# A hybrid encoder layer: DeltaNet decays by repeated row reads, two products in f16 parts, the gate projection spread through the chunks, gates ahead of the normalising

## The chip, the cores and the metric

The kernel runs on one core of one Trainium2 chip. The metric is the device time of one execution in microseconds, the median of the runs shown; lower is better.

## The reference, cut to what matters

One layer of an encoder trunk (1024 tokens, width 1024): four mixers read one projection of the normalised input, their outputs are gated and merged, then come cross attention to a memory of 256 tokens and a mixture of 32 experts. The change touches the fourth mixer, a bidirectional gated DeltaNet (4 heads of width 64), and the merge.

```python
def gdn_scan(q, k, v, beta, log_a):
    gam = jnp.cumsum(gc, axis=-1)
    diff = gam[..., :, None] - gam[..., None, :]
    decay = jnp.exp(jnp.where(incl, diff, -jnp.inf))
    kk = jnp.einsum('bhntd,bhnsd->bhnts', kc, kc)
    a_mat = jnp.where(strict, bc[..., None] * kk * decay, 0.0) + jnp.eye(c)
    rhs = jnp.concatenate([vc * bc[..., None], kc * (bc * jnp.exp(gam))[..., None]], axis=-1)
    sol = lax.linalg.triangular_solve(a_mat, rhs, left_side=True, lower=True, unit_diagonal=True)
    qk = jnp.einsum('bhntd,bhnsd->bhnts', qc, kc) * decay
    q_dec = qc * jnp.exp(gam)[..., None]
    def step(state, inp):
        v_new = u_i - jnp.einsum('bhtd,bhde->bhte', kc_i, state)
        o = jnp.einsum('bhtd,bhde->bhte', qd_i, state) + jnp.einsum('bhts,bhse->bhte', qk_i, v_new)
        state = cd_i[..., None, None] * state + jnp.einsum('bhsd,bhse->bhde', kd_i, v_new)
...
def gdn_mixer(...):
    o = rmsnorm(o_f + o_b, norm_g) * jax.nn.silu(z)
...
def gated_merge(h, branches, merge_w, merge_b, branch_up):
    for i, y in enumerate(branches):
        term = jax.nn.sigmoid(h @ merge_w[i] + merge_b[i]) * (y @ branch_up[i])
        out = term if out is None else out + term
```

## The kernel before

The whole layer is one program. `plan_schedule` writes out one list of steps by hand, and each engine walks through this list in order and does its share of each step; between engines there are only semaphore waits. Each engine, and each engine's own DMA queue, is thus in order.

**Dense work.** Every large product is a panel of weights, 256 columns wide, named by what it makes: `nz` is the DeltaNet's output gate projection z, `merge20` to `merge23` the merge of the third mixer, `early1` and `early2` the middle merge gates of the fourth, `merge30` its first two tiles (gates and `up` products), `late3` the `up` products of the middle tiles, `merge33` the last two tiles. Weights are split into two f16 parts, and each product is three f16 matmuls. For this SyncE loads two rows of weight tiles (a chunk, "conv") into one of four landing slots (L1260), ScalarE makes the high part (L1358), VectorE (or GpSimd in some panels) the low part (L1944). The chunks of a panel are spread through the parts of the panel before it; the first stands ahead of its first part. A part is 6 matmuls of 128x512 or 12 of 128x256. Every group of four parts fills one of two PSUM banks, used in turn, and the next user of a bank waits until it has been emptied ("evac"): a gate by ScalarE with a tanh (L1379), an `up` product by VectorE. `dense(..., between=...)` puts the parts into a list: each `None` in `between` is a place for one part, every other entry is a step of the mixers.

**DeltaNet.** 8 chunks of 128 tokens, two directions `d` of 4 heads. `gdn_gam` makes the running sums of the log decays and their exponentials. `gdn_a` i makes for chunk i the decayed blocks: part 0 forms the differences of the running sums by one f32 product with a triangular matrix (L979; GpSimd writes its right side at L2793) and the exponential (L1707), GpSimd masks it (L2799), part 1 makes the key and query products (L989) which VectorE scales (L2367, L2375), part 2 a transpose (L996) and copies of the diagonal blocks (L1715). The blocks go to memory (L1747) and are read back later. `gdn_inv` are steps of VectorE (L2385, L2388) that invert the 32x32 diagonal blocks of half the chunks; 10 such steps for the first half stand in and behind the last `gdn_a`, 10 for the second half in the first three `gdn_c`. `gdn_c` i has seven parts:

- 0: the decay of the queries by a product (GpSimd L2820, TensorE L1014, exponential L1725), GpSimd spreads the inverted blocks into block matrices (L2807), first level of the inverse (L1023), negated by VectorE (L2406)
- 1 to 3: the other products of the inverse (L1033, L1040, L1023), copied by VectorE and ScalarE
- 4: its product with the keys (L1047)
- 5: its product with the values, f32 (L1053), less that with the state (L1061); VectorE scales the new values
- 6: the state's addition (L1067), the output from the state (L1072) and from the new values, f32 (L1075); VectorE updates the state (L2429) and adds the output (L2432; for the first four chunks ScalarE stores it)

After the recurrence `fin` squares, sums and normalises the output (VectorE's gain product is L2227), `fin_gate` multiplies by silu of the `nz` result (L2235), `fin_tr` transposes it (L889) into Y, which the `up` products of the fourth mixer read. `early_in` makes SyncE wait for the gain product and then read back eight stored gates (L1281), which the `late3` evacuations use.

## Time and profile before

| | us |
|---|---|
| median of 3 runs (2063.43 to 2067.67) | 2064.29 |
| the profiled execution, its own time | 2065.67 |
| its span, first to last instruction | 2063.9 |
| TensorE busy | 1909.5 |
| VectorE busy | 1388.5 |
| ScalarE busy | 1083.7 |
| GpSimd busy | 324.1 |

The mean granted TensorE clock was 0.971 of full speed. Busy is the time that at least one instruction of an engine covers; as matmuls are pipelined, the time that a group of them costs is read from the chain, which gives their issue times. An f32 matmul has two records. The stretches: `gdn_a` some 673 to 754 us, `gdn_c` 792.3 to 954.9 us, `nz` to 975.8 us, `merge30` from there.

### The profile page before, as it was taken

Reading aid. Unit: us, or ns where it says so; the run is one execution under the profiler, and the core shown is the slowest. Engines: PE = TensorE matmul, PEld = TensorE weight load, DVE = VectorE, ACT = ScalarE, POOL = GpSimd, SP = SyncE. Lnnn points to the kernel's source line nnn. Section 1 sums busy time; section 2 is a strip of 40 time slices with the busy share of each in tenths; the row PEclk is TensorE's granted clock in tenths of the full one; section 3 lists DMA queues with packets and bytes.
Section 4 is the critical chain, followed back from the end, with each engine's and each line's share of the span. In section 5 each row is a group of like instructions: output and inputs, shape, how many; then the busy total and the mean of one; then the engine's idle time right before and its main releaser. Section 6 shows DMA issues by size and latency. Waiting matters only on the chain.

```text
span 2063.9 us, 33015 instructions
## 1 busy us (share of the span) xinstructions
PE 1909.5 (93%) x13076; PEld 1138.2 (55%) x13076; DVE 1388.5 (67%) x1831; ACT 1083.7 (53%) x1582; POOL 324.1 (16%) x285
## 2 busy tenths in 40 slices
PE   6999999999999999999999999895899999999991
PEld 3464565655544545767488855685355444444440
DVE  4555533799865687634643845437799999999986
ACT  4563223666656432223333534334588888888862
POOL 6000100344300523421000000000001111111102
PEclk9999999999999999999999999997899999999995
DMA  5411111212011352332321500403799999999976
GB/s 185 161 51 42 32 42 53 66 47 57 24 39 47 118 179 83 113 108 99 138 67 48 168 32 21 167 31 152 268 423 422 422 422 421 422 422 422 422 290 261
DMA packets 140522, 360.45 MB, mean 175 GB/s; under 512 B 38224, under 2 KB 91632, under 8 KB 113776
## 3 DMA queue, kind: packets, MB, share of 16 engines
q1 hardware_dynamic: 96608, 279.57, 35.7%
q10 hardware_dynamic: 34944, 46.14, 6.4%
q0 software_dynamic: 8848, 33.03, 4.1%
q8 instruction: 87, 1.43, 0.3%
q14 instruction: 35, 0.29, 0.0%
HBM read 307.85 MB, written 46.66 MB: 172 GB/s over the span
## 4 chain that ended last, share of the span: by engine, by line
PE 79%; DVE 9%; ACT 5%; issue 4%; DMA 1%; SPq 1%; DVEq 0%; ACTq 0%; POOL 0%; POOLq 0%
PE psum L787 40%; PE psum L1194 24%; ACT arena L1636 2%; PE psum L1183 1%; PE psum L1118 1%; PE psum L1093 1%; DVE arena L2288 1%; PE psum L917 1%; PE psum L1212 1%; PE psum L804 1%; PE psum L1053 1%; PE psum L989 1%; DMA arena<-in_w_in_dram 1%; PE psum L979 1%; PE psum L928 1%
## 5 line engine op out<-in xcount | busy, mean ns | idle before, releaser
L787 PE MATMUL psum<-arena 128*128 128x512 f16 (+2 forms) x6000 | 1016.6, 327 | 7.7 <-issue 2.8
L787 PEld LDWEIGHTS psum<-arena 128*128 128x128 f16 x6000 | 569.6, 98 | 391.5 <-issue 23.5
L1194 PE MATMUL psum<-arena 128*128 128x512 f16 x2304 | 513.5, 382 | 15.6 <-issue 12.5
L744 DVE SCALAR_TENSOR_TENSOR arena<-arena 128x2048 f16<-128x2048 f32 x192 | 437.6, 2286 | 57.9 <-ACT arena L738 57.6
L738 ACT ACTIVATE arena<-arena 128x2048 f16<-128x2048 f32 x192 | 365.5, 1908 | 69.6 <-DMA arena<-in_w_dram 42.9
L1194 PEld LDWEIGHTS psum<-arena 128*128 128x128 f16 x2304 | 224.7, 98 | 282.4 <-issue 24.7
L1944 DVE SCALAR_TENSOR_TENSOR arena<-arena 128x512 f16<-128x512 f32 (+1 forms) x185 | 124.9, 695 | 123.0 <-ACT arena L1358 122.6
L2847 POOL DMA_INDIRECT arena<-xhat,arena x32 | 67.5, 2109 | 842.1 <-PE psum L1183 446.0
L1358 ACT ACTIVATE arena<-arena 128x512 f16<-128x512 f32 (+1 forms) x212 | 127.0, 616 | 35.8 <-PE psum L787 11.4
L1379 ACT ACTIVATE arena<-psum,arena 128x512 f32<-128x512 f32 x64 | 43.8, 684 | 149.2 <-PE psum L787 149.1
L1443 ACT ACTIVATE arena<-psum 128x512 f32<-128x512 f32 (+3 forms) x51 | 29.9, 586 | 119.8 <-PE psum L787 119.8
L1407 ACT ACTIVATE arena<-arena 128x256 f32<-128x256 f32 x64 | 26.6, 416 | 108.9 <-DVE arena L1980 107.9
L2735 POOL TENSOR_SCALAR arena<-arena 128x512 f32<-128x512 f32 x27 | 57.5, 2129 | 138.8 <-ACT arena L1358 138.8
L2273 DVE CUSTOM_DVE_ANT_0 arena<-psum,arena 128x1024 f32<-128x1024 f32 x64 | 75.6, 1219 | 2.1 <-PE psum L904 2.0
L1968 DVE SCALAR_TENSOR_TENSOR arena<-arena,psum 128x512 f32<-128x512 f32 x64 | 43.8, 684 | 49.0 <-PE psum L787 34.8
L1636 ACT ACTIVATE arena<-arena 128x1024 f32<-128x1024 f32 x64 | 72.9, 1147 | 7.1 <-DVE arena L2273 7.0
L1998 DVE SCALAR_TENSOR_TENSOR arena<-psum,arena 128x512 f16<-128x512 f32 x36 | 24.8, 690 | 61.5 <-ACT arena L1443 31.0
L1980 DVE SCALAR_TENSOR_TENSOR arena<-psum,arena 128x512 f32<-128x512 f32 x32 | 22.1, 690 | 64.3 <-PE psum L787 64.3
L1645 ACT ACTIVATE arena<-psum 128x512 f16<-128x512 f32 x64 | 34.7, 595 | 55.1 <-PE psum L917 34.3
L2807 POOL TENSOR_TENSOR arena<-arena 128x512 f32<-128x512 f32 x32 | 34.8, 1106 | 128.0 <-DMA arena<-gdn_inv 82.6
L1859 ACT ACTIVATE arena<-psum 128x512 f32<-128x512 f32 x64 | 38.1, 597 | 14.2 <-PE psum L1194 13.9
L1183 PE MATMUL psum<-arena 128*128 128x128 f32 x256 | 34.4, 278 | 10.3 <-DMA arena<-xhat,arena 10.3
(390 smaller groups left out, 2089.6 us busy)
## 6 DMA issues: line engine op xcount, KB each, us to landing
arena<-in_w_dram SPq DMA_DIRECT2D x192, 1024.0 KB, 11.9
arena<-in_merge_w_dram SPq DMA_DIRECT2D x64, 256.0 KB, 3.0
yrows<-arena ACTq DMA_DIRECT2D x32, 512.0 KB, 7.9
arena<-in_w_in_dram SPq DMA_DIRECT2D x48, 256.0 KB, 2.8
gdn_lq<-arena ACTq DMA_DIRECT2D x8, 1024.0 KB, 4.0
arena<-gdn_lq ACTq DMA_DIRECT2D x8, 1024.0 KB, 5.1
arena<-in_xattn_wkv_dram SPq DMA_DIRECT2D x32, 256.0 KB, 2.8
yrows<-arena POOLq DMA_DIRECT2D x1, 7680.0 KB, 24.3
```

What stands on the lines that cost most here:

```text
L738: nc.scalar.activation(half_of(pieces(e, m)[0], half), half_of(XLAND[m], half), ACT.Copy, scale=WS).then_inc(w_hi[m], 1)
L744: nc.vector.scalar_tensor_tensor(half_of(lo, half), half_of(XLAND[m], half), WS, half_of(hi, half), ALU.mult, ALU.subtract).then_inc(w_lo[ ...
L787: mm = nc.tensor.matmul(bank[prt[0]:prt[1], c0:c1], lhs[a](k), rhs[b](k), start=(k == 0 and a + b == 0), stop=(k == nk - 1 and a == 1))
L1183: tr = nc.tensor.transpose(PS[:, k // 4, (k % 4) * P:(k % 4) * P + P], xs[:, k, :], ident)
L1194: mm = nc.tensor.matmul(PS[:, bank, :], left[a][:, k, :], right[b][:, k, columns], start=k + a + b == 0, stop=(k == n - 1 and a == 1))
L1358: S.activation(W[i % 2][0][:, 2 * j:2 * j + 2, 0:wide], LAND[c % NLAND][:, :, 0:wide], ACT.Copy, scale=WS).then_inc(*act_hi.mark(c))
L1379: S.activation(SG[gate_no[n] % 2], bank, ACT.Tanh, scale=0.5 / WS, bias=half_b[:, 8 * kind[1] + kind[2]:8 * kind[1] + kind[2] + 1]).then_i ...
L1636: S.activation(DS[u % 2][:, m, :], DS[u % 2][:, m, :], ACT.Exp, scale=-1.0, bias=d_mx[u % 2][:, m:m + 1], accum_out=d_l[u % 2][:, m:m + 1])\
L1944: V.scalar_tensor_tensor(W[i % 2][1][:, 2 * j:2 * j + 2, 0:wide], LAND[c % NLAND][:, :, 0:wide], WS, W[i % 2][0][:, 2 * j:2 * j + 2, 0:wid ...
L2273: V.tensor_tensor_reduce(out=DS[u % 2][:, m, :], in0=PS[:, 2 + 2 * m:4 + 2 * m, :].rearrange("p a b -> p (a b)"), in1=DWH[:, 896 - P * qt: ...
L2735: G.tensor_scalar(landed_c, landed_c, WS, None, ALU.mult).then_inc(*counter("pool_w_scaled").mark(chunk))
L2847: G.indirect_dma_start(XR[e % 2], None, XH_D, bass.IndirectOffsetOnAxis(IDX[:, e:e + 1], 0)).then_inc(rows_in[e % 2], 16)
```

## The change

1. **Decays.** A new step `gdn_rows` transposes the running sums (64 rows of 128), and ScalarE writes them and their exponentials to memory. `gdn_a` part 0 no longer has a product: DMAs of ScalarE's queue read the four rows of a chunk and direction into all 128 partitions, ScalarE makes Relu(column - row) per head and the exponential of its negative. `gdn_first` issues the first reads, the others are issued two chunks ahead. In `gdn_c` part 0 four DMAs per chunk bring the exponentials of the rows for the queries; VectorE waits for them in part 4. GpSimd's L2793 and L2820, and TensorE's L979 and L1014, are gone.
2. **f16 parts.** The products of the inverse with the values (part 5) and of the decayed scores with the new values (part 6) become three f16 matmuls each. Their operands are split: ScalarE makes the high, VectorE the low parts (`zh`, `zl`, `qh`, `ql`, `vh`, `vl` per chunk and direction, the values once). The output's products move behind the state products of both directions, and the state's update waits only for the latter (`qs`).
3. **Order.** `nz` is no longer a stretch of its own: `gdn_a` 0 to 5 and `gdn_c` get 16 more places. The panel merge30 has its four gates first and then its four `up` products; they begin at once after the recurrence, with `fin_tr` after 11 of their parts. The four gates go where the stored gates would go, not into the two slots. `early_in` waits for the gating product instead of the gain product. `merged_pair` 0 moves from merge30 to merge33.

```diff
-PAIRS_AT = {(3, 1, 0, 2): [(0, 2)], (3, 6, 0, 1): [(1, 2)], ...
+PAIRS_AT = {(3, 6, 0, 0): [(0, 2)], (3, 6, 0, 1): [(1, 2)], ...
...
-            if (i, q) != (3, 0):
+            if (i, q) == (3, 0):
+                pairs = pairs[::2] + pairs[1::2]
+            else:
...
-        gdn += [("gdn_a", i, 1)] + {...}.get(i, []) + [None] + [("gdn_a", i + 1, 0), None] * (i + 1 < TT) + mid
+        gdn += [("gdn_a", i, 1)] + {...}.get(i, []) + [None] * (1 + (i < 6)) + [("gdn_a", i + 1, 0), None] * (i + 1 < TT) + mid
...
-            gdn += [("gdn_c", i, part)] + [None] * (1 <= part < 6)
+            gdn += [("gdn_c", i, part)] + [None] * (part < 6 + (i < 2))
...
-    dense("nq", "nk", "nv", *merge(2), *[f"early{q}" for q in (1, 2)], between=gdn)
-    dense("nz", between=[("fin", "gdn")])
-    order += [("fin_gate", "gdn"), ("early_in",)]
+    dense("nq", "nk", "nv", *merge(2), *[f"early{q}" for q in (1, 2)], "nz", between=gdn)
...
-    dense(*merge(3), between=[None] * 4 + [("fin_tr", "gdn"), ("mem_again",)] + [None] * 16 + [("mem_stats",)] + again)
+    dense(*merge(3), between=[("fin", "gdn"), ("fin_gate", "gdn"), ("early_in",)] + [None] * 11 + [("fin_tr", "gdn"), ("mem_again",)]
+          + [None] * 12 + [("mem_stats",)] + again)
...
-                            nc.tensor.matmul(B0[:, :, :], st_f if d else st_b, NX[d], start=True, stop=True)\
-                                .then_inc(*q.mark("seg", i, d))
...
-                                nc.tensor.matmul(PS[:, 3 + 3 * d, h * 64:h * 64 + 64], NZ_[d][:, SLOT_OF[h], :],
-                                                 NVT[:, c, h * 64:h * 64 + 64], start=h == 0, stop=False)
+                                for x, y in ((0, 0), (0, 1), (1, 0)):
+                                    nc.tensor.matmul(PS[:, 3 + 3 * d, h * 64:h * 64 + 64], NZP[d][x][:, SLOT_OF[h], :],
+                                                     NVP[y][:, c, h * 64:h * 64 + 64], start=h + x + y == 0, stop=False)
...
+                            mm.then_inc(*q.mark("qs", i, d))
+                    if part == 6:
+                        for d in range(2):
+                            pe.wait_ge(*v.at("ql", i, d))
+                            pe.wait_ge(*v.at("vl", i, d))
                             for h in range(NH):
+                                for x, y in ((0, 0), (0, 1), (1, 0)):
+                                    mm = nc.tensor.matmul(PS[:, 2 + 3 * d, h * 64:h * 64 + 64], NQP[s][d][x][:, SLOT_OF[h], :],
...
-                    sp.wait_ge(*counter("vec_fin").at("g", "gdn"))
+                    sp.wait_ge(*counter("vec_fin").at("done", "gdn"))
...
+                            act.wait_ge(gam_in[i % 2], 32 * (i // 2) + 32)
+                            for h in range(NH):
+                                S.activation(NGR[i][d][:, h, :], NGR[i][d][:, h, :], ACT.Relu, scale=-1.0, bias=GAS[:, d, c, h:h + 1])\
...
+                            S.activation(NY[d], NGR[i][d], ACT.Exp, scale=-1.0).then_inc(*a.mark("dt", i, d))
...
+                                S.activation(NZP[d][0], NZ_[d], ACT.Copy, scale=WS).then_inc(*a.mark("zh", i, d))
...
+                            S.activation(NNP[d][0], NVN[d], ACT.Copy).then_inc(*a.mark("vh", i, d))
...
+                            S.activation(NQP[i % 2][d][0], NQT[i % 2][d], ACT.Copy, scale=WS).then_inc(*a.mark("qh", i, d))
...
+                            V.scalar_tensor_tensor(NZP[d][1], NZ_[d], WS, NZP[d][0], ALU.mult, ALU.subtract).then_inc(*v.mark("zl", i, d))
...
+                            V.scalar_tensor_tensor(NQP[i % 2][d][1], NQT[i % 2][d], WS, NQP[i % 2][d][0], ALU.mult, ALU.subtract).then_inc(*v.mark("ql", i, d))
...
+                            V.tensor_tensor(NNP[d][1], NVN[d], NNP[d][0], ALU.subtract).then_inc(*v.mark("vl", i, d))
...
+                S.activation(early_gate(kind), bank, ACT.Tanh, scale=0.5 / WS, ...
```

## Rows read from the trace of the kernel before

**Rows 1.** The page: busy us, share and instructions of each engine.
```profile
PE 1909.5 (93%) x13076; PEld 1138.2 (55%) x13076; DVE 1388.5 (67%) x1831; ACT 1083.7 (53%) x1582; POOL 324.1 (16%) x285
```

**Rows 2.** Busy times by stretch: length, then busy us (instructions) of each engine.
```profile
673.00:752.00 79.00, 76.69 (x515) 42.85 (x514) 55.19 (x86) 35.95 (x88) 39.81 (x32) 1.00 0.38 131
...
790.00:955.00 165.00, 155.09 (x1791) 114.53 (x1790) 93.03 (x246) 39.08 (x91) 58.59 (x79) 0.99 0.29 86
```

**Rows 3.** The chain that ended last, 950 to 1400 us: start, us, what.
```profile
954.86 20.97 PE psum L787 x192
...
979.71 2.30 DVE arena L2235
```

**Rows 4.** Timeline of all engines, 948 to 992 us: start, duration, what.
```profile
955.50 0.42 DVE L2432 TENSOR_TENSOR arena<-psum,arena 128x256 f32<-128x256 f32 x1
...
966.91 3.67 SPq L1281 DMA_DIRECT2D arena<-early_gates  x8
...
970.63 0.80 SPq L1260 DMA_DIRECT2D arena<-in_branch_up_dram  x1
...
979.58 0.61 ACT L1358 ACTIVATE arena<-arena 128x512 f16<-128x512 f32 x1
...
981.04 0.69 ACT L1379 ACTIVATE arena<-psum,arena 128x512 f32<-128x512 f32 x1 [0.84 <-PE psum L787]
...
982.05 1.97 PE L889 MATMUL psum<-arena 128*128 128x128 f32 x16 [1.05 <-DVE arena L2235]
```

**Rows 5.** TensorE's waits, 790 to 992 us.
```profile
PE psum L1033 <- DVE arena L2406: 4.4, 8, 1.5
```

**Rows 6.** The chain that ended last, 560 to 955 us: start, us, what.
```profile
573.33 0.70 PE psum L928 x24
...
681.94 1.72 PE psum L979 x4
...
805.19 0.84 PE psum L1053 x8
...
812.68 0.50 PE psum L1014 x4
```

**Rows 7.** TensorE's instructions by line, 790 to 955 us.
```profile
L1075 PE MATMUL psum<-arena 128*128 128x64 f32 x128 | 16.1, 268 | 0.0
```

**Rows 8.** Busy times, last two chunks of `gdn_a`.
```profile
731.00:754.00 23.00, 19.89 (x137) 11.17 (x136) 20.49 (x39) 8.89 (x23) 7.28 (x6) 1.00 0.26 104
```

**Rows 9.** ScalarE's instructions by line, 673 to 955 us.
```profile
L1715 ACT ACTIVATE arena<-arena 32x128 f32<-32x128 f32 x32 | 9.8, 307 | 0.8
```

**Rows 10.** Timeline of GpSimd and VectorE, 731 to 800 us.
```profile
733.24 2.50 POOL L2793 TENSOR_TENSOR arena<-arena 128x512 f32<-128x512 f32 x2
...
733.77 1.02 DVE L2385 TENSOR_TENSOR arena<-arena 128x30 f32<-128x30 f32 x1
...
758.19 0.69 DVE L1944 SCALAR_TENSOR_TENSOR arena<-arena 128x512 f16<-128x512 f32 x1
...
798.56 0.20 DVE L2385 TENSOR_TENSOR arena<-arena 128x30 f32<-128x30 f32 x1
```

**Rows 11.** Busy times of the first four chunks of `gdn_c`.
```profile
792.30:812.50 20.20, 18.70 (x223) 13.97 (x223) 15.61 (x41) 4.54 (x11) 9.77 (x13) 1.00 0.06 19
812.50:833.00 20.50, 18.96 (x224) 14.10 (x224) 17.98 (x45) 5.01 (x12) 6.91 (x9) 1.00 0.28 78
833.00:854.00 21.00, 19.03 (x224) 14.17 (x224) 16.69 (x45) 5.54 (x13) 7.75 (x11) 1.00 0.35 102
854.00:874.00 20.00, 19.53 (x228) 14.69 (x227) 8.52 (x24) 6.14 (x14) 8.74 (x14) 1.00 0.49 159
```

**Rows 12.** DMAs that read branch_up weights, 940 to 1000 us.
```profile
DMA to landing us min/median/max: 3.0/6.3/7.5
```

**Rows 13.** Busy times, 2 us in `gdn_c` after a wait; the column PEclk.
```profile
895.00:897.00 2.00, 1.61 (x64) 1.38 (x66) 1.32 (x6) 0.38 (x1) 0.72 (x2) 1.00 0.03 8
897.00:899.00 2.00, 2.00 (x24) 0.86 (x15) 1.30 (x5) 0.00 (x0) 0.00 (x0) 0.54 0.00 0
```

174 lines of the change are left out of this document (105 added, 69 removed).

## The prediction

> **What bounds it now.** I read the page first: TensorE is busy for 93% of the span [rows 1]. The edits lie between 673 us and 992 us, so the busy times by stretch come next: in the stretch that forms the decays and the triangular blocks, TensorE works 76.7 us of 79; in the stretch of `gdn_c`, 155.1 of 165; VectorE is at 93.0 of 165 there, as a mean [rows 2]. By the chain, the recurrence ends at 954.86 us, the `nz` projection then takes 20.97 us of unbroken TensorE work, and of the normalising only a 1.05 us wait for the gating product is left open in front of `fin_tr` [rows 3, 4]. So TensorE bounds this part: a matmul taken out shortens it, one moved does not, and idle time is worth filling only where there is some. By the list of waits, the largest in `gdn_c` is 4.4 us behind VectorE's negated blocks, among 9.9 us of idle in all (165 less 155.1) [rows 2, 5].
>
> **What is taken out of TensorE.** The prices are issue times of the chain [rows 6]. The segment sum in `gdn_a` costs 1.72 us per chunk (two of 128x512 f32, four records), 13.8 us over 8 chunks. The decay product in `gdn_c` costs 0.50 us per direction, 16 times: 8.0 us. The two f32 products against 64-column values cost 0.84 us per direction for 8 records; 128 records of the second [rows 7], as many of the first (8 chunks, 2 directions, 4 heads, 2 records), make 16 groups each, 32 x 0.84 = 26.9 us. In their place stand 12 f16 matmuls of the same 128x64 shape per group; the chain has 24 of them in 0.70 us, so 0.35 us, 32 times: 11.2 us. The new transpose is one matmul. Net: 13.8 + 8.0 + 26.9 - 11.2 = 37.5 us less TensorE work.
>
> The segment sum's two weight loads lie inside the 1.72 us. The Trainium skill (TensorE: Matmul & The Clock Gate, Weight-path perf modes) says that fast weight load is off for FP32, which is why the f16 form can gain by more than its three products lose; the trace agrees (0.84 against 0.35 us), and by the page alone the sum would be the same.
>
> **What is moved.** The 16 parts of `nz` (1.31 us each, 20.97 / 16) go into 6 new places in `gdn_a` and 10 in `gdn_c`. That is the same TensorE work; it gains only where it falls on idle time. `gdn_a` then changes per chunk by 1.31 - 1.72 = -0.4 us, for six chunks -2.5 us; in the last two VectorE is the busy one (20.5 of 23 us, [rows 8]), so the 3.4 us of their segment sums I take as nothing, with -3 us as the other end. `gdn_c` 0 begins at 792.3 - 2.5 = 789.8 us.
>
> The decays now come by repeated reads. In `gdn_a` ScalarE gains eight Relu of 128x128 and two DMA issues per chunk. The nearest row for a small activation is 0.31 us [rows 9], so some 3 us a chunk, 25 us on an engine that has 36 of 79 us busy [rows 2]; the rows are read two chunks (18 us) ahead. I cost this at nothing; if that cover failed, each chunk would wait some 2 us, 16 us in all. GpSimd loses `tla` and `lab`, which is slack it had; its cost to VectorE is weighed below.
>
> **`gdn_c`, the disputed term.** Before, 8 chunks took 162.6 us (792.3 to 954.86). Without 8.0 + 26.9 - 11.2 = 23.7 us and with 10 places of 1.31 us it is 152.0 us if the waits stay. They will not stay. VectorE gets six new operations per chunk: four low halves of 128x512 at 0.69 us [rows 10] and two of 128x256 at about 0.4 [rows 4], or 3.5 us. The first three chunks, which also hold the inverses of the second half, have VectorE at 15.6, 18.0 and 16.7 us of 20.2 to 21 [rows 11]: 19.1, 21.5 and 20.2 after. TensorE would need only 19.9, 20.2 and 19.4 us. VectorE is late there, and with the handoffs that an engine at its limit cannot hide (today 1.5 to 2 us per chunk) I take 20.9, 22.6 and 21.5 = 65.0 us. In the last five (VectorE 8.5 + 3.5 us in the row of the first of them, of some 18.4) TensorE leads: 100.9 before (854.0 to 954.86), less 5 x 2.96 = 14.8, plus 6.5 = 92.6, and for the two new handoffs (values to f16 on ScalarE, the rest on VectorE, both ahead of the state update in VectorE's order) 0.5 us a chunk: 95.1. Together 160 us. From both sides: 142 us if even the old waits vanish (152.0 - 9.9); 172 us if VectorE's added 28 us all fall on the path and the new places absorb only 8 of them.
>
> Here a rule speaks against the change. The rows show an operation of 30 elements on VectorE taking 1.02 us where the same form takes 0.20 us, and the long one stands while GpSimd multiplies [rows 10]. The Trainium skill (SBUF — State Buffer, Who interferes with whom) says that a VectorE operation with two SBUF inputs and a GpSimd operation that reads SBUF exclude each other for the whole instruction. All six new low halves have two SBUF inputs, and those of the values come while GpSimd spreads the blocks of the next chunk. By row one such meeting costs 0.8 us; two a chunk would be 13 us over the stage, the upper half of my bound, while the loss of `tla` and `lab` gives some back.
>
> **The end of the recurrence, where a new wait appears.** After it, the order is `fin`, `fin_gate`, `early_in`, and then the gates of merge30 with 11 places before `fin_tr`. Let E be the end of the last product, 789.8 + 160 = 949.8 us. VectorE's part as now: the last sum 1.06 us after E; from there to the early-gate reads, which now stand behind the gain product, 11.0 us (966.91 less 955.92) [rows 4]. In the new order they stand behind the gating product too, 2.3 us more [rows 3]: E + 14.4. Eight issues take 3.67 us: E + 18.0. Only then can SyncE issue the next panel's weights, late3 chunk 0, which is behind them in its order. The same pair today: issued at 970.63, and the landings of this tensor take 3.0 to 7.5 us, the middle one 6.3, behind the 2 MB of gates [rows 4, 12]. So the weights land at E + 24.3.
>
> On ScalarE the conversion of that chunk stands ahead of the tanh of the first gate (it is the first step of merge30's first part). So the first bank is empty at E + 24.3 + 0.6 + 0.7 = E + 25.6 [rows 4]. TensorE fills two banks in 8 parts, 8 x 1.31 = 10.5 us, and must then wait: 15.1 us. Queued behind it: two gates, `fin_tr`, everything. Before, this order did no harm, because `nz` covered the time in which VectorE normalised and loads went out. On top: after a far shorter gap (1.6 of 2 us busy) the granted clock stood at 0.54 for the next 2 us [rows 13], so for most of it the lower of the levels 1.2 and 2.4 GHz; some 4 us at it would cost 2 us, which I add. `fin_tr` itself is then no longer waited for (-1.05).
>
> **Sum.** Before, the gates of merge30 begin at 954.86 + 20.97 = 975.83, with 1.05 us to wait: 976.9. After: 949.8 + 15.1 + 2 = 966.9. Gain 10.0 us against the profiled execution of 2065.67 us (span 2063.9): 2055.7. That execution lies 1.4 us over the median of 2064.29, so 2054.3 us; I say 2055. Everything after merge30 waits for it, so the gain arrives whole. The eighth pair (`merged_pair` 0) in merge33 costs ScalarE and VectorE about a microsecond each beside gates of 5 us: nothing.
>
> **Rivals.**
> (a) The hold behind `early_in` does not come or is short (the weights land as soon as the first landings do, or SyncE is released earlier). For it: TensorE had no such hold in the trace. Against: one queue each on SyncE and ScalarE, both in order. Then 2055 - 17 = 2038 us.
> (b) Slower: VectorE becomes the bound of all of `gdn_c`, by the low halves and their exclusion by GpSimd. The change breaks even when 976.9 = 789.8 + C + 17.1, that is at C = 170.0 us, 21.3 a chunk against 20.3 now. For it: the first chunks have VectorE nearly full. Against: the later ones have it below half. At C = 175, 2070 us. By the skill's exclusion rule alone C is 160 + 13 = 173, 2067 us.
> (c) The fill is worth nothing and the products gain nothing, because waits take their place one for one, the hold included: near 2064 us. What speaks for it is that each freed microsecond in `gdn_c` lies next to a handoff; against, that 13.8 us of segment sums have no new handoff on TensorE.
>
> **How the numbers follow.** Forecast (hold and C of 150 to 166) 0.64, its own range 2045 to 2061; (a) 0.14; (b) 0.13; (c) 0.09. About 0.2% (4 us) is what a measurement of this kernel can tell from no change. Faster takes the forecast nearly whole and (a), 0.77; the same 0.10; slower 0.13. The range reaches to (a), and to C = 172: 2037 to 2067.
>
> **What would show it.** After the recurrence: a gap on TensorE of about 15 us, eight parts behind its end, with ScalarE's conversion waiting for a branch_up DMA; no gap refutes it. `gdn_c`: about 160 us, its first three chunks longer than the rest, VectorE over 90% in them, f16 groups of 12 in about 0.35 us. `gdn_a`: no f32 128x512 product, chunks of 9.0 us. I am wrong if ScalarE is late with the Relus, if the row reads land late, or if the hold is not there.

## The result and the profile after

The changed kernel takes 2082.94 us (median of 5 runs, 2078.02 to 2087.12) against 2064.29 us (median of 5 runs beside it, 2063.22 to 2071.28): a ratio of 1.0084, 95% interval 1.0059 to 1.0110. It is slower by 0.8%, where 2055 us was forecast with a range of 2037 to 2067. The profiled execution is the longest of the five, 2087.12 us (span 2085.4); the one of before took 2065.67. One execution of experiment e9 took 8630.36 us, against 2054.86 to 2063.89 us of the other eight, and is left out of its ratio.

The page first: busy us and share of each engine, as in [rows 1].

```profile
PE 1888.3 (91%) x13109; PEld 1117.6 (54%) x13109; DVE 1424.9 (68%) x1883; ACT 1121.1 (54%) x1680; POOL 302.0 (14%) x253
```

TensorE does 21.2 us less and the kernel takes 21.5 us more, so some 43 us of idle time are new. The busy times by stretch say where. Columns as in [rows 2]; the stretches are `gdn_a`, the first two intervals of `gdn_c`, its third, the rest of it, and the time after the recurrence.

```profile
678.50:801.10 122.60, 108.02 (x679) 58.28 (x678) 84.20 (x153) 63.37 (x168) 27.10 (x23) 0.96 0.56 175
801.10:849.00 47.90, 37.37 (x450) 24.56 (x450) 42.62 (x97) 15.44 (x33) 12.62 (x14) 0.92 0.25 69
849.00:876.00 27.00, 20.73 (x245) 14.10 (x245) 20.62 (x51) 7.87 (x17) 7.40 (x8) 0.88 0.30 90
876.00:980.70 104.70, 94.20 (x1306) 72.07 (x1306) 67.00 (x148) 37.41 (x80) 31.20 (x36) 0.92 0.31 94
980.70:1004.00 23.30, 10.35 (x48) 4.51 (x46) 10.50 (x8) 8.16 (x9) 0.00 (x0) 0.80 0.41 134
```

The columns are the stretch, its length, the busy us (and instructions) of TensorE, its weight loads, VectorE, ScalarE and GpSimd, then TensorE's granted clock and two columns on DMA. TensorE is idle for 14.6 of the 122.6 us of `gdn_a`, for 27.3 of the 179.6 us of `gdn_c` and for 13 us right after it. VectorE is busy for 63.2 of the first 74.9 us of `gdn_c` (84%) and for 67.0 of the other 104.7 us (64%). The list of TensorE's waits, 670 to 1015 us (what waits, for whom: us in total, times, longest), names the holders:

```profile
PE psum L1071 <- DVE arena L2474: 15.4, 3, 6.3
PE psum L797 <- ACT arena L1382: 13.0, 1, 13.0
PE psum L996 <- ACT arena L1753: 8.7, 5, 2.3
PE psum L1026 <- DVE arena L2496: 8.1, 3, 3.4
PE psum L1003 <- DVE arena L2427: 5.9, 1, 5.9
PE psum L1049 <- ACT arena L1775: 2.2, 4, 0.9
PE psum L1085 <- DVE arena L2493: 0.6, 1, 0.6
```

Before, the largest was 4.4 us in eight pieces [rows 5]. L1071 (the state's addition, L1067 before) waits for VectorE's new values (L2474), three times: in the chunks that hold the inverses. L1026 (first level of the next chunk's inverse) waits for VectorE's sum of the output (L2496), since it writes the bank that the sum reads. L996 (the key products of `gdn_a`) waits for ScalarE's diagonal copies (L1753), and L1003 (its transposes), once, in the last chunk, for VectorE's scaled products (L2427); these two make up the 14.6 us of `gdn_a`. L797 is dense work, the gates of merge30; its one wait of 13.0 us is the hold.

These measures repeat below, all from the traces: `gdn_a`, from its first key product to the first product of the inverse in `gdn_c`; `gdn_c`, from there to E, the end of its last output product; inside it the seven intervals between the starts of the eight chunks' products with the state (L1076); and "to the router", from the first key product to a product of the expert routing behind all edits (L1161, L1151 before), 751.2 us before and 769.9 us after. They scatter: the changed kernel, e1 and e2 have the same code in `gdn_c` and show 179.4, 177.2 and 175.4 us, so that a difference of 2 to 4 us in `gdn_c` between two traces says little by itself.

| us | before | after | forecast |
|---|---|---|---|
| `gdn_a` | 114.4 | 122.6 | 111.3 |
| `gdn_c` | 161.7 | 179.4 | 160 |
| E to the gates (`nz` included before) | 22.0 | 0 | 0 |
| hold and slow clock behind it | 0 | 13.0 + 2.1 | 15.1 + 2 |

The forecast's 111.3 us is 789.8 less 678.5 us; its 160 us counts from 792.3 us in the kernel before, where the stage is 162.6 us long.

**The hold**, in the chain that ended last (start, us, what):

```profile
981.57 1.92 ACT arena L1613
...
983.51 2.30 DVE arena L2265
...
986.44 2.30 DVE arena L2267
...
988.77 2.30 DVE arena L2274
...
991.17 2.30 DVE arena L2282
993.48 0.35 SPq L1291
...
997.20 5.56 DMA arena<-in_branch_up_dram
...
1003.32 0.68 ACT arena L1382
```

The last output group ends at 980.53 us. VectorE's gating product ends at 993.47, SyncE then issues eight reads of early gates (L1291) and only then the next panel's weights, which land at 1002.76; ScalarE converts them ahead of the first gate's tanh (L1382). TensorE fills its two banks and stands from 991.05 to 1004.04.

**A late chunk of `gdn_c`**, the timeline of all engines (start, duration, what):

```profile
953.90 4.91 POOL L2862 TENSOR_TENSOR arena<-arena 128x512 f32<-128x512 f32 x4 [12.99 <-PE psum L1065]
...
954.58 0.76 DVE L2474 SCALAR_TENSOR_TENSOR arena<-psum,arena 128x256 f32<-128x256 f32 x2
...
955.49 2.42 DVE L2493 TENSOR_TENSOR arena<-arena 128x256 f16<-128x256 f32 x2
...
957.62 0.94 PE L1085 MATMUL psum<-arena 128*128 128x64 f16 x24
957.83 0.41 DVE L2479 TENSOR_TENSOR arena<-psum,arena 128x256 f32<-128x256 f32 x1
...
958.27 0.94 DVE L2484 SCALAR_TENSOR_TENSOR arena<-arena 128x128 f32<-128x128 f32 x2
...
960.60 0.74 DVE L2496 SCALAR_TENSOR_TENSOR arena<-psum,arena 128x256 f32<-128x256 f32 x2
...
961.11 0.97 PE L1026 MATMUL psum<-arena 32*32 32x32 f32 x32 [2.55 <-DVE arena L2496]
```

From the new values (954.58) everything up to the next chunk's first product stands in VectorE's order: low halves (L2493), masks and state (L2479, L2484), sums (L2496). TensorE's output products (L1085) are done by 958.6 us, and it then stands for 2.55 us. The pair of low halves takes 2.42 us while GpSimd spreads blocks (L2862).

### The profile page after: what moved, and what is told of

Same layout as the page of the kernel before. It is cut to its first block, busy times and chain, and to the rows that moved or that the text cites. A ratio compares the mean times of both kernels' runs of the same rounds, so it can differ in the third digit from the quotient of the medians.

```text
span 2085.4 us, 33231 instructions
## 1 busy us (share of the span) xinstructions
PE 1888.3 (91%) x13109; PEld 1117.6 (54%) x13109; DVE 1424.9 (68%) x1883; ACT 1121.1 (54%) x1680; POOL 302.0 (14%) x253
## 4 chain that ended last, share of the span: by engine, by line
PE 75%; DVE 11%; ACT 6%; issue 5%; DMA 2%; SPq 1%; DVEq 1%; ACTq 0%; POOLq 0%
PE psum L797 38%; PE psum L1204 24%; ACT arena L1650 2%; PE psum L1193 1%; PE psum L1128 1%; PE psum L1103 1%; DVE arena L2335 1%; PE psum L927 1%; PE psum L996 1%; PE psum L1222 1%; PE psum L814 1%; DVE arena L2437 1%; DVE arena L2440 1%; ACT arena L1735 1%; DMA arena<-in_w_in_dram 1%
## 5 line engine op out<-in xcount | busy, mean ns | idle before, releaser
L797 PE MATMUL psum<-arena 128*128 128x512 f16 (+2 forms) x6000 | 1022.8, 328 | 20.9 <-ACT arena L1382 13.0
L797 PEld LDWEIGHTS psum<-arena 128*128 128x128 f16 x6000 | 570.9, 99 | 406.3 <-issue 22.6
L1204 PE MATMUL psum<-arena 128*128 128x512 f16 x2304 | 513.7, 382 | 15.1 <-issue 12.0
L1368 ACT ACTIVATE arena<-arena 128x512 f16<-128x512 f32 (+1 forms) x212 | 127.3, 616 | 64.1 <-issue 15.4
L1394 ACT ACTIVATE arena<-psum,arena 128x512 f32<-128x512 f32 x60 | 41.1, 684 | 133.3 <-PE psum L797 133.1
L2027 DVE SCALAR_TENSOR_TENSOR arena<-psum,arena 128x512 f32<-128x512 f32 x32 | 22.1, 690 | 64.6 <-PE psum L797 64.6
L2862 POOL TENSOR_TENSOR arena<-arena 128x512 f32<-128x512 f32 x32 | 38.1, 1219 | 128.1 <-DMA arena<-gdn_inv 67.1
## 6 DMA issues: line engine op xcount, KB each, us to landing
yrows<-arena POOLq DMA_DIRECT2D x1, 7680.0 KB, 24.3
```

Of the source, the lines that this page charges most:

```text
L797: mm = nc.tensor.matmul(bank[prt[0]:prt[1], c0:c1], lhs[a](k), rhs[b](k), start=(k == 0 and a + b == 0), stop=(k == nk - 1 and a == 1))
L1204: mm = nc.tensor.matmul(PS[:, bank, :], left[a][:, k, :], right[b][:, k, columns], start=k + a + b == 0, stop=(k == n - 1 and a == 1))
L1368: S.activation(W[i % 2][0][:, 2 * j:2 * j + 2, 0:wide], LAND[c % NLAND][:, :, 0:wide], ACT.Copy, scale=WS).then_inc(*act_hi.mark(c))
```

## The experiments

Ratios are to the kernel before, measured beside each run on the same chip, with 95% intervals. The quotient of the two medians can lie up to 0.23% beside the ratio; where that matters it is given too. Two kernels are compared by their ratios; many of these pairs come from different chips, and the changed kernel's 1.0084 was measured apart from the experiments. "Base" is the kernel that an edit is made to.

### Each suspect of the change by itself (base: the changed kernel)

**e1**: the early gates' reads stand nine parts later.

```diff
-    dense(*merge(3), between=[("fin", "gdn"), ("fin_gate", "gdn"), ("early_in",)] + [None] * 11 + ...
+    dense(*merge(3), between=[("fin", "gdn"), ("fin_gate", "gdn")] + [None] * 9 + [("early_in",)] + [None] * 2 + ...
```

> The changed kernel with one step moved: SyncE's wait for the gating product (early_in) stands behind nine parts of merge30 instead of ahead of them, so that both weight chunks of the next panel are issued before it. Theory (the 13.0 us gap behind the recurrence is this order alone): the wait of TensorE for the tanh of the first gate goes from 13.0 us to under 1 us, and the time falls from 2083 to about 2070 us. Rival (the gap would be there anyway, because VectorE is still normalising): a wait of about the same length stands in front of the transposes, and the time falls by less than 4 us.

Measured: 0.9998 [0.9982, 1.0014]. The wait for L1382 is gone from the list, the others stay within 1 us. By ratio the hold is worth 0.86%, some 18 us, for a wait of 13.0 us and 2.1 us of slow clock behind it; from E to the router the traces are 18.3 us apart. The 3 us beyond the priced 15.1 were not traced.

**e2**: ScalarE's Relus and exponentials of the next chunk behind the diagonal copies.

```diff
-  ... [("gdn_a", i + 1, 0), None] * (i + 1 < TT) + mid
-        gdn += [("gdn_a", i, 2), ("gdn_out", i)]
+  ... [None] * (i + 1 < TT) + mid
+        gdn += [("gdn_a", i, 2)] + [("gdn_a", i + 1, 0)] * (i + 1 < TT) + [("gdn_out", i)]
```

> The changed kernel with ScalarE's share of gdn_a part 0 (eight Relu, two exponentials, two row reads) moved behind the copies of the diagonal blocks of the chunk before; TensorE's order is the same, as part 0 has no product any more. Theory (TensorE's 8.7 us of waits for those copies come from the Relus ahead of them in ScalarE's order): gdn_a takes about 9 us less, 2074 us. Rival (ScalarE's total is the bound of gdn_a, so the wait only changes its place: the masks of GpSimd come later and VectorE's scaling waits for them): within 3 us of 2083.

Measured: 1.0084 [1.0058, 1.0109] (by the medians 1.0075), `gdn_a` 121.9 us: the 9 us are not there. Its list of waits has no L996 any more, but the wait at L1003 grew from 5.9 to 11.2 us: the decays come late instead.

```profile
PE psum L1003 <- DVE arena L2427: 11.2, 5, 6.7
```

This order took no work off ScalarE's queue, it only chose what is late.

**e3** and **e4**: one product back in f32, with all of its parts, waits and scales: the output's in e3 (first edit), the values' in e4 (second).

```diff
-                                for x, y in ((0, 0), (0, 1), (1, 0)):
-                                    mm = nc.tensor.matmul(PS[:, 2 + 3 * d, h * 64:h * 64 + 64], NQP[s][d][x][:, SLOT_OF[h], :],
+                                mm = nc.tensor.matmul(PS[:, 2 + 3 * d, h * 64:h * 64 + 64], NQT[s][d][:, SLOT_OF[h], :],
...
-                                for x, y in ((0, 0), (0, 1), (1, 0)):
-                                    nc.tensor.matmul(PS[:, 3 + 3 * d, h * 64:h * 64 + 64], NZP[d][x][:, SLOT_OF[h], :],
+                                nc.tensor.matmul(PS[:, 3 + 3 * d, h * 64:h * 64 + 64], NZ_[d][:, SLOT_OF[h], :],
```

> The changed kernel with the output's product (decayed scores with new values) back in f32: without qh, ql, vh, vl, with 6.7 us more of TensorE work (16 groups at 0.84 instead of about 0.42 us). Theory (VectorE's order and its exclusion by GpSimd's spreading bound gdn_c): gdn_c falls from 179.6 us to about 168, the pair of low halves of the new values that took 2.42 us is gone, 2071 us. Rival (TensorE bounds gdn_c): 2090 us.

> The changed kernel with the product of the inverse with the values back in f32: without zh, zl and the low half of the values, with 6.7 us more of TensorE work. Theory (what hurts is low halves on VectorE where it is full or meets GpSimd; zl stands in part 3, while TensorE has two parts to do): a small gain in the first three chunks, about as much lost in the last five, 2078 to 2084 us. Rival one (every low half costs its full time, 1.4 us a chunk, and the conversions of ScalarE too): 2072 us. Rival two (TensorE bounds): 2090 us.

Measured: e3 1.0029 [1.0016, 1.0043], `gdn_c` 167.7 us (168 forecast); e4 1.0056 [1.0035, 1.0077], `gdn_c` 174.3 us, between its theory and its first rival. TensorE as the bound is refuted in both. The output's f16 form is a loss; for the values' form the interval overlaps the changed kernel's, and it alone is less sure.

### Taken together, and the order alone

**e5**: both products in f32 (the edits of e3 and e4). **e6**: e5 with the edit of e1. **e7**: the kernel before with only the new order (nz spread, gates first, kept gates). **e8**: e7 with the edit of e1.

> The changed kernel with both 64-column products back in f32 (no f16 parts of either; the row reads, the spread of the gate projection and the new order after the recurrence stay). Theory 1 (f16 parts are a loss here, because the matmul time they save is less than the VectorE and ScalarE work and the handoffs they put ahead of TensorE's next step, and the two losses are separate): the two single reversals add up, 0.55% and 0.28% below the changed kernel, so a ratio to the kernel before of about 1.000, and gdn_c falls from 179.6 to some 162 us. Rival 2 (the losses have one common cause, a VectorE that is full in the first chunks, so that taking either product's parts away already removes it): no more than the larger single one, a ratio near 1.003. Rival 3 (the f16 form does save once VectorE is free): the ratio is above 1.003.

> As the run before it, and the reads of the early gates stand behind nine more parts of merge30, so that SyncE issues the next panel's weights first. Theory 1 (the hold is 13 us whatever the recurrence does): 13 to 17 us less than the run before it, a ratio near 0.992, some 2040 us against 2056 before, and the wait for ScalarE's tanh of the kept gate is gone. Rival (with the recurrence shorter the reads are issued earlier and the hold was shorter already): less than 8 us between the two.

> The kernel before with only the new order: the gate projection nz spread through the chunks, the gates of merge30 over the normalising, the kept gates; decays by products and both products in f32 as before. Theory 1 (spread parts fill only the idle time there is, 9.9 us in gdn_c, and the hold behind early_in costs 13 us): nz's 21 us cost the recurrence some 14 to 16 us, the hold 13: slower than before by about 6 us, ratio 1.001 to 1.005. Rival 1 (the spread parts fill nothing): 12 us slower, 1.006. Rival 2 (the hold does not come without the row reads): ratio 0.995 to 0.998.

> The run before it with the early gates' reads later. Theory 1: 13 us less, so some 7 us below the kernel before, ratio 0.996 to 0.998. Then the difference between this run and e6 is what the row reads for the decays bring alone: by the matmul time they save 21.8 us, by the 8.7 us of waits for ScalarE in gdn_a and its longer chunks about 8 us; if e6 is not below this run, the row reads bring nothing.

| | ratio | `gdn_a`, us | `gdn_c`, us | L1071 or its like, us | hold, us |
|---|---|---|---|---|---|
| e5 | 1.0003 [0.9992, 1.0014] | 123.1 | 168.1 | 4.4 | 12.5 |
| e6 | 0.9953 [0.9929, 0.9977] | 122.9 | 168.0 | 3.9 | 0 |
| e7 | 1.0071 [1.0047, 1.0095] | 120.8 | 173.2 | 5.8 | 13.6 |
| e8 | 0.9985 [0.9971, 0.9999] | 121.4 | 172.1 | 5.0 | 0.4 |

By ratio the two single reversals add up (0.55% and 0.28%, together 0.81%), as theory 1 said; in `gdn_c` they don't (168.1 us, no shorter than e3's 167.7, and 162 was forecast). Whether the values' parts cost anything without the output's is thus open. The hold is worth 0.50% from e5 to e6, 10 us where 13 to 17 were forecast, and 0.86% from e7 to e8; from E to the router the traces give 14.1 and 14.8 us. The order alone is slower by 0.7% (0.1 to 0.5% forecast), and the hold is all of it: without it e8 is no slower than before. Sixteen parts of `nz` lengthen `gdn_a` by 6.4 and `gdn_c` by 11.5 us, 17.9 of their 21: spreading them filled 3 us. e6 to e8, where neither has a hold, gives the row reads 0.3% (by the traces 2.8 us to the router), e5 to e7 0.7% (3.7 us); the intervals overlap, and neither is the 21.8 us of matmuls that they remove.

### What in the f16 form costs

**e9** (base: the changed kernel): GpSimd's spreads cut to one column for chunks 3 to 7; part of the blocks is left out.

```diff
+                            if i < 3:
                                 spread(NX[d], d, d).then_inc(*po.mark("x", i, d))
                                 spread(NZ_[d], 1 - d, d).then_inc(*po.mark("z", i, d))
+                                continue
+                            G.tensor_copy(NX[d][:, :, 0:1], XZC[s][:, 8 * d + 4 * d:8 * d + 4 * d + 4, 0:1]).then_inc(*po.mark("x", i, d))
+                            G.tensor_copy(NZ_[d][:, :, 0:1], XZC[s][:, 8 - 4 * d:12 - 4 * d, 0:1]).then_inc(*po.mark("z", i, d))
```

> The changed kernel, but for the last five chunks of gdn_c GpSimd's four spreads of the next blocks (1.23 us each) are cut to a copy of one column, so that this part of the blocks is left out of the computation. Theory 1 (GpSimd's spread and VectorE's low half of the values exclude each other, the pair takes 2.42 us in place of 0.84, and VectorE's order behind it sets when the next chunk's y may start): the pair takes 0.8 to 0.9 us in these chunks, the wait of L1026 for DVE falls by about 1.5 us a chunk, gdn_c by 6 to 8 us from 179.4, ratio about 1.005. Rival (VectorE is not what sets the end there, or the pair is long for another reason): pair and gdn_c stay, ratio 1.008.

Measured: 0.9984 [0.9969, 0.9999], `gdn_c` 161.4 us, 18.0 less and over twice the forecast. The same pair and the first state updates in its timeline, and two of its waits:

```profile
938.62 0.76 DVE L2493 TENSOR_TENSOR arena<-arena 128x256 f16<-128x256 f32 x2 [0.15 <-ACT arena L1785]
...
940.14 0.61 DVE L2484 SCALAR_TENSOR_TENSOR arena<-arena 128x128 f32<-128x128 f32 x2
```
```profile
PE psum L1071 <- DVE arena L2474: 11.5, 3, 4.5
...
PE psum L1026 <- DVE arena L2496: 3.4, 3, 1.2
```

The pair takes 0.76 us in place of 2.42 us, so GpSimd's work was what stretched it. The Trainium skill (SBUF — State Buffer, Who interferes with whom) says that an operation with two SBUF inputs and a GpSimd operation that reads SBUF lock each other out for the whole instruction. The trace agrees: beside the last spread (to 958.81 us) the changed kernel's mask, with one input in PSUM, took 0.41 us, against 0.42 here, while the pair of state updates behind it, with two SBUF inputs, took 0.94 us against 0.61 here. But the stretched pairs make up only 2 us a chunk; how 18.0 us come of them is not shown by this run.

**e10** (base: the changed kernel): f16 output product of high halves alone, the low halves left out.

```diff
-                            pe.wait_ge(*v.at("ql", i, d))
-                            pe.wait_ge(*v.at("vl", i, d))
+                            pe.wait_ge(*a.at("qh", i, d))
+                            pe.wait_ge(*a.at("vh", i, d))
...
-                            V.scalar_tensor_tensor(NQP[i % 2][d][1], NQT[i % 2][d], WS, NQP[i % 2][d][0], ALU.mult, ALU.subtract)...
-                            V.tensor_tensor(NNP[d][1], NVN[d], NNP[d][0], ALU.subtract)...
...
```

> The changed kernel with the output product still as 12 f16 matmuls a group, but all of the high halves; the four low halves of it (two of 128x512, two of 128x256 on VectorE) are left out. Theory 1 (VectorE's low halves and what is queued behind them are the loss): gdn_c falls by more than the 11.7 us that the f32 form brought, since the shorter f16 group stays: 162 to 166 us, ratio 1.001 or below. Rival (ScalarE's high halves and the longer chain of handoffs from the values to the group are the loss): gdn_c stays above 172 us, ratio above 1.005.

Measured: 1.0038 [1.0024, 1.0051], `gdn_c` 169.8 us: between the two. Leaving out the low halves gives 9.6 of the 11.7 us that the f32 form brings. This kernel still has f16 groups that are 0.49 us shorter than e3's, 7.8 us over 16 groups, and yet it is no shorter than e3. By subtraction ScalarE's high halves and the handoffs behind them cost some 10 us; no run cuts them alone.

**e11** (base: the changed kernel): VectorE's sums ahead of masks and state.

```diff
+                    for d in range(2 * (part == 6 and i >= 4)):
+                        dve.wait_ge(*q.at("o", i, d))
+                        V.scalar_tensor_tensor(NO[:, c, :], PS[:, 2 + 3 * d, 0:256], 1 / WS, NO[:, c, :], ...
```

> The changed kernel with one order changed: in the chunks in which VectorE adds the output (the last four), the two sums stand ahead of the masking and the state update in its order, not behind them. Theory 1 (the bank of the next y is free late, since the sum waits behind 2.9 us of masking and state update, which themselves wait behind the low halves): the 8.1 us of waits of L1026 for the sum fall to under 3 us, gdn_c by 3 to 5 us, ratio about 1.006. Rival (the state update is as urgent: GpSimd's products with it come late and hold the next chunk): the wait moves to the state or the key products, no gain, 1.008.

Measured: 1.0050 [1.0032, 1.0068], `gdn_c` 170.7 us, 8.7 less (3 to 5 forecast). The last three intervals fall from 21.4, 21.8 and 22.2 to 19.0, 18.8 and 19.2 us; the first two stay at 27.0 and 26.9. L1026 waits for the sum no more; 3.3 us of waits turned up at the next product of the inverse (L1035), and the state was not urgent. The hold grew from 13.0 to 15.0 us, so that 6.2 us of the 8.7 are left at the router (0.34%, 7 us, by ratio).

**e13** (base: the changed kernel): the parts formed, the f32 product used without waiting for them, its scale left out.

> The changed kernel in which all f16 parts of the output product are still formed, but the product is the f32 one of 8 records a group and waits for none of them (the scale of that product is left out, so the output is not the reference's). Theory 1 (VectorE's operations for the parts delay the mask, the state and the next chunk whether the product waits for them or not): gdn_c stays within 4 us of the changed kernel's 179.4, ratio 1.007 to 1.010. Rival (it is the product's wait for the low halves, and the parts by themselves would be hidden): gdn_c falls towards the 167.7 of the f32 form, ratio below 1.005.

Measured: 1.0076 [1.0052, 1.0101] (by the medians 1.0090), `gdn_c` 184.8 us: 5.4 us above the changed kernel, where at most 4 us were forecast, with 7.8 us of longer products in it. The rival is refuted: the work for the parts delays the chunk whether or not the product waits for it.

**e17** (base: e6): the cut of e9 where there are no output or value parts.

> The kernel of e6 (both products f32, early gates read later), GpSimd's spreads cut in the last five chunks as in e9 (part of the blocks is left out of the computation). Theory 1 (the 18 us of e9 come of the exclusion and VectorE's order, which bind only with the low halves): gdn_c within 3 us of e6's 168.0. Rival (the spreads load VectorE and the clock whatever the product's form): gdn_c falls by 6 us or more, to 162 or less.

Measured: 0.9893 [0.9872, 0.9913], `gdn_c` 159.5 us, 8.5 less than e6. The forecast of 3 us was wrong, the rival's 6 us or more came. Its last four intervals are 19.6, 19.2, 19.2 and 19.2 us against e6's 19.6, 19.4, 19.8 and 19.8: 1.4 us. Almost all the rest falls in the second and third (24.6 and 24.2 to 20.9 and 21.1), and one wait accounts for half of it:

```profile
PE psum L1069 <- DVE arena L2453: 3.9, 1, 3.9
```
```profile
PE psum L1069 <- DVE arena L2453: 0.6, 1, 0.6
```

(e6, then e17.) There VectorE has the inverses to do and meets the spread of the first cut chunk. In the last four intervals of the f16 form the same cut had given 12.2 us (84.0 less 71.8). I read this so: GpSimd's spreads cost VectorE time in both forms, and it reaches the end only where VectorE's order is what the next chunk waits for: in the inverse chunks, or everywhere once the f16 parts are in it. That fits both runs; a spread that is moved instead of cut would test it.

### Row reads, Relus, and the best form of each

**e12** (base: e6): `gdn_a`'s decays by the segment-sum product again, `gdn_c`'s by row reads.

```diff
+                        if part == 0:
+                            pe.wait_ge(*po.at("tla", i, d))
+                            nc.tensor.matmul(B0[:, :, :], st_f if d else st_b, NX[d], start=True, stop=True)...
-                                S.activation(NGR[i][d][:, h, :], NGR[i][d][:, h, :], ACT.Relu, ...
-                            S.activation(NY[d], NGR[i][d], ACT.Exp, scale=-1.0)...
+                            S.activation(NY[d], PS[:, 2 + 3 * d, :]..., ACT.Exp)...
```

> The kernel of e6 (both products f32, early gates read later) with gdn_a's decays by the segment-sum product again, as before the change; gdn_c's still come by row reads. Theory 1 (in gdn_a the row reads gain nothing, since the 13.8 us of products are replaced by waits for ScalarE's Relus): within 3 us of e6, either side, ratio 0.994 to 0.997, and TensorE is busy in all of gdn_a's first chunks of 10.7 to 10.9 us. Rival (the product's matmuls did bound gdn_a): 8 to 14 us slower than e6, ratio about 1.000.

Measured: 0.9942 [0.9924, 0.9961], `gdn_a` 123.1 us, e6 has 122.9. Taking 13.8 us of products out of `gdn_a` was worth nothing. What the row reads bring is in `gdn_c`, 166.3 us here against 172.1 in e8, with 8.0 us of products gone.

**e15** (base: e6): the Relus' work on GpSimd.

```diff
-                                S.activation(NGR[i][d][:, h, :], ..., ACT.Relu, scale=-1.0, bias=GAS[:, d, c, h:h + 1])...
+                            G.tensor_tensor(NGR[i][d], NGR[i][d], bc(GAS[:, d, c_, :]...), ALU.subtract)...
+                            G.tensor_scalar(NGR[i][d], NGR[i][d], 0.0, None, ALU.min)...
```

> The kernel of e6 (both products f32, early gates read later) with the lower bound of the differences formed on GpSimd (a subtraction and a minimum of 128x512 a direction) in place of ScalarE's eight Relus a chunk. Theory 1 (the Relus ahead of the diagonal copies in ScalarE's order are what lengthens gdn_a): the 8.7 us of waits of L996 for ScalarE go, gdn_a's chunks fall from 10.9 to 9.5 us or less, 6 to 9 us less than e6, ratio 0.991 to 0.993. Rival (GpSimd and VectorE exclude each other here, and VectorE is late in its place): PE waits for VectorE's products, gdn_a no shorter, ratio 0.995 or above.

Measured: 0.9893 [0.9864, 0.9922], `gdn_a` 118.8, `gdn_c` 165.3. The medians, 2042.96 us against 2060.34, give 0.9916. Of the kernels that compute the whole layer it has the lowest ratio, but e18's interval overlaps its own and e18's medians give the same 0.9916. By its list of waits L996 waits for ScalarE once, and VectorE is next:

```profile
PE psum L1003 <- DVE arena L2406: 6.1, 3, 5.0
...
PE psum L996 <- ACT arena L1745: 3.3, 1, 3.3
```

`gdn_a` gave 4.1 us, not the 6 to 9 forecast, and `gdn_c` 2.7; to the router it is 6.8 us shorter than e6. GpSimd is busy for 70.7 us of `gdn_a` in place of 27.3, and VectorE, with as many instructions (153), for 92.4 in place of 84.1: the rival's wait was there too (L1003), at a price smaller than the gain.

**e14** (base: the changed kernel): e1's and e11's edits, and f16 output only from chunk 3 on. **e16**: e14 without row reads in `gdn_a`. **e18**: e14 with e15's edit.

```diff
+                                if i < 3:
+                                    mm = nc.tensor.matmul(PS[:, 2 + 3 * d, h * 64:h * 64 + 64], NQT[s][d][:, SLOT_OF[h], :],
...
+                                    continue
```

> The changed kernel with three edits: early gates read later, the output sums first in VectorE's order, and the output product in f16 parts only from chunk 3 on, in f32 in the three chunks that hold the inverses. Theory 1 (in those chunks VectorE is full, and each operation added there is added to the path; in the others the low halves are hidden once the sums come first): the first two intervals between the chunks' products fall from 27.0 and 26.8 to about 22 and 24.5, as in the f32 form, the later ones stay at 19; gdn_c 163 to 166 us, ratio 0.990 to 0.994. Rival (the f16 values are what holds the first chunks): the first intervals stay above 25, gdn_c about 170, ratio 0.996.

> The kernel of e14 with gdn_a's decays by the segment-sum product, as before the change. Theory 1 (the row reads are neutral there): within 3 us of e14. Rival: 5 us or more slower, since TensorE's 13.8 us come back.

> The kernel of e14 (f16 values everywhere, f16 output from chunk 3 on, sums first, early gates read later) with the lower bound formed on GpSimd as in e15. Theory 1 (the f16 parts bring nothing even with everything else mended, since their shorter groups are paid with VectorE's and ScalarE's work): within 4 us of e15's ratio of 0.9893, either side. Rival (the f16 parts' 0.4 us a group show once nothing else is in the way): 5 to 8 us below e15, ratio about 0.986.

Measured: e14 0.9954 [0.9924, 0.9985], `gdn_c` 169.1 us, first intervals 25.4 and 24.3; e16 0.9979 [0.9959, 0.9998]; e18 0.9921 [0.9903, 0.9939], `gdn_c` 165.5 us. e14 was forecast at 163 to 166 us and 0.990 to 0.994. The second interval came as forecast, the first (22 forecast) did not; it is 24.6 in e16 and 22.2 in e18, as in e3 (22.1), so it isn't the f16 values, and its cause was not found. e16 lies 5 us above e14 by ratio, with overlapping intervals, and 0.8 us by the traces to the router: between its theory and its rival the runs don't decide. e18 was forecast within 4 us of e15 and is 5.8 us above it by ratio, again with overlapping intervals, and 0.1 us by the traces to the router (733.8 against 733.7); the rival, f16 5 to 8 us ahead, is refuted. Even with all that was found mended, f16 parts end where f32 does (169.1 against 168.0, 165.5 against 165.3). The f32 forms never had the sums first, which might have helped them too.

## Why the prediction was wrong

Three steps failed. "A matmul taken out shortens it", by which TensorE alone bounds this part; "I cost this at nothing" for ScalarE's new work in `gdn_a`, which came out 11.3 us later than forecast; and the 160 us of `gdn_c`, which took 179.4, because VectorE's order between two chunks was priced at 0.5 us of handoffs. The hold, the price of the f16 groups and the clock behind the hold were right.

**What TensorE is relieved of.** Right as a price: the chain of the changed kernel has the f16 group at 0.35 us.

```profile
952.94 0.35 PE psum L1057 x12
```

But 37.5 us less matmul work showed as 21.2 us less busy time. Up to the end of the recurrence the granted clock is 0.88 to 0.96 in the stretches above, against 1.00 and 0.99 in [rows 2]; two waits behind which dense work ran slower are shown below. The step "a matmul taken out shortens it" is the first that failed: it holds only as long as nobody else is as late as TensorE, and here ScalarE and VectorE were. e12 shows it plainly: with or without the 13.8 us of segment sums `gdn_a` takes 123 us. Rival (c) had this mechanism, and what the prediction set against it, that the segment sums had no new handoff, is what failed.

**`gdn_a`: "I cost this at nothing".** The cover failed: 122.6 us in place of 111.3, where the sentence behind it had priced a failure at 16 us, and chunks of 10.1 to 12.4 us in all but the last interval, in place of 9.0. The Relu takes 0.387 us, not 0.31, and eight of them with two exponentials are 4.4 us a chunk ahead of the diagonal copies in ScalarE's order. ScalarE's listing for 678 to 755 us:

```profile
L1735 ACT ACTIVATE arena<-arena 128x128 f32<-128x128 f32 x60 | 19.0, 387 | 2.2 <-PE psum L797 2.2
L1740 ACT ACTIVATE arena<-arena 128x512 f32<-128x512 f32 x16 | 10.1, 630 | 0.5
```

The busy share (36 of 79 us) was read as slack. What counted is that TensorE waits once a chunk for this one queue, and that the new work stands between; put behind the copies (e2) it makes the decays late instead. e15 shows it in part, with 4.1 us back when the Relus leave ScalarE; 5.0 us of its remaining waits are one wait for VectorE. What else made up the 11.3 us is open. That the read rows would land late was refuted: no wait for them stands in the lists of TensorE's waits.

**`gdn_c`: 160 us, bounds 142 to 172; it took 179.4.** The failed term. The two intervals 820.49 to 874.28 were forecast at 22.6 and 21.5, and measured 27.0 and 26.8 us: 9.7 over. The last five were forecast at 95.1 and took 104.2: 9.1 over. The ends (19.4 us up to the first state product, 2.0 behind the last) came near the 20.9 us of the first chunk. Two things were mis-sized. In the first chunks the new VectorE work was added to its busy time with 1.1 to 1.8 us for the handoffs, as if VectorE would be over 90% busy; it was busy for 84%, and TensorE waited all the same for the new values in front of the state's addition (15.4 us in three chunks, where [rows 5] had no such wait). In the last ones 0.5 us a chunk stood for the handoffs; the low halves (9.6 us over the stage by e10), the values' pair trebled by GpSimd's spreads (12.2 us by e9's last four intervals), stood in front of the sums, and those in front of the next chunk (8.7 us by e11). These overlap: they are three ways to shorten one chain. "The later ones have it below half" held for the kernel before only (41.1 of 100.9 us). The prediction's own sum, 8.5 + 3.5 us of 18.4, makes 65%, and it came to 64% (67.0 of 104.7 us). But neither share would have shown the wait: it comes of the order.

**The rule that spoke against the change** gave 173 us and 2067 us for the whole; it was the nearer one. Its price was right too: the prediction took 0.8 us for a meeting, and the pair shows (2.42 - 0.76) / 2 = 0.83 us for each of two. Rival (b), to which it belongs, is what happened in its outcome, C (the length of `gdn_c`) above the break-even of 170.0 us; VectorE held the chunks by its order, though, and not by a full load. It got 0.13.

**The hold: right.** 13.0 us (15.1 forecast) and 2.1 us of clock: 18 dense matmuls take 6.12 us behind the hold and 4.06 us in e18, where the wait is 1.4 us.

```profile
1004.04 6.12 PE L797 MATMUL psum<-arena 128*128 128x512 f16 x18 [12.99 <-ACT arena L1382]
```
```profile
969.00 4.06 PE L797 MATMUL psum<-arena 128*128 128x512 f16 x18 [1.41 <-ACT arena L1388]
```

The weights land at E + 22.2 (24.3 forecast): VectorE's gating product ends at E + 12.9 in place of 14.4, and the landing takes 5.6 in place of 6.3 us. Rival (a) is refuted. What the hold costs in the end, 18 us by e1 and 10 and 18 us by the two other pairs of kernels with and without it, is known less well than its length.

**The sum** with the measured terms: gates free to go at 980.5 + 13.0 + 2.1 = 995.6 us against 976.9, 18.7 us later, and 18.7 us is also what the traces differ by at the router. The medians differ by 18.65 us, but the two profiled executions by 21.5; the rest arose behind the router, where nothing was edited, so that part of the agreement with the medians is luck. Of the 18.7 us, 19.4 us are `gdn_c` over its forecast and 11.3 us `gdn_a` over its own, against the 10.0 us that were to be gained, and 2.0 us less hold.

**Still open.** How the f16 loss divides between lock-out, length of VectorE's order and ScalarE's halves can't be read as a sum, since the cuts overlap, and single traces of `gdn_c` scatter by up to 4 us. The row reads' own worth is 0.3 to 0.7% by ratio and 2.8 to 3.7 us by the traces. A later spread on GpSimd, in place of a cut one, wasn't tried, nor the sums first with products in f32.

## What to carry to other kernels

Before counting what a matmul saves, follow one buffer round its loop: which engine's order lies between a bank's last reader and its next writer, and what would the change put into it; in such a loop an engine that is busy for two thirds of the time still sets the pace. When work is cheap because an engine looks idle, find what stands behind it in that engine's queue (here moving the Relus from ScalarE to GpSimd gave 0.6% by ratio, 6.8 us by the traces). And whoever moves a load behind longer work should list what stands behind the load in its queue: one step moved by nine places was worth 0.5 to 0.9%.

## What the hardware showed unexpectedly

- GpSimd's spreads cost more than the operations they visibly stretch: the pair of low halves is 1.7 us longer beside them, some 8 us over the five chunks, but cutting 20 spreads (1.23 us each) gave 18.0 us in the f16 form and 8.5 us in the f32 form.
- The granted clock was 0.88 to 0.92 across `gdn_c` with TensorE busy for 77 to 90% of it, and 1.00 in the first 48 us of it in e12, where it was busy for 97%:

```profile
801.00:849.00 48.00, 46.55 (x566) 31.37 (x566) 39.49 (x103) 11.77 (x26) 14.30 (x17) 1.00 0.28 78
```

So idle time was paid for twice: by the chain a group of 12 dense f16 matmuls of 256 columns takes 1.31 us at 954.69 us, and after the wait of 2.55 us that ends at 961.11 us it took

```profile
962.08 2.67 PE psum L797 x12
```

- ScalarE's issue of four row-read DMAs took 2.40 us (958.17 to 960.57), during which it computed nothing, where two took 0.81 and 0.98 us in `gdn_a`.
